# First norm taken by tokens beside the first projection tile, last norm split into a weight per tile and a factor per token

## The reference, cut to what matters

```python
def first_block(...):
    h = concatenate([meta_tokens, x], axis=1)        # 16 + 512 rows of 1024
    for i in range(2):
        hn = _rmsnorm(h, norm_attn[i])               # i == 0: the first norm
        h = h + mixer(hn, ...)                       # i == 0: starts with hn @ w_in_even
        h = h + _sq_relu_mlp(_rmsnorm(h, norm_mlp[i]), ...)
    return _rmsnorm(h, norm_final)[:, 16:]

def second_block(...):
    h = hybrid_layer(x, ...)     # ends: h = h + sigmoid(h @ w_ple_gate) * (p @ w_ple_proj)
    return rmsnorm(h, g_final)                       # the last norm

def rmsnorm(x, g):
    return x * rsqrt(mean(x * x, axis=-1) + EPS) * g
```

## Time and profile before

| | us |
|---|---|
| median of 3 runs | 2258.49 (2254.37 to 2258.91) |
| the profiled execution, its own time | 2258.82 |
| its span, first to last instruction | 2257.0 |
| PE busy | 2178.8 (97%) |
| POOL / DVE / ACT busy | 896.0 / 1167.3 / 788.6 |
| mean granted TensorE clock | 0.989 |

### The profile page before, as it was taken

How to read it: one execution, slowest core, us unless ns; L and a number is a source line. 1 busy time by engine, 2 the same in 40 slices (tenths; PEclk the granted TensorE clock), 3 DMA queues, 4 the chain that set the end, 5 groups by cost and what they waited for, 6 DMA issues and landing times.

```text
span 2257.0 us, 33166 instructions
## 1 busy us (share of the span) xinstructions
PE 2178.8 (97%) x13070; PEld 1837.5 (81%) x13070; DVE 1167.3 (52%) x1764; ACT 788.6 (35%) x1329; POOL 896.0 (40%) x404
## 2 busy tenths in 40 slices
PE   7999899999999989999999989999999999999996
PEld 6987699999999756788887878788878788887874
DVE  5558757742752266651154358656564554442224
ACT  3338733212323275332233322234423332222223
POOL 2321734333444344444444433333334444444442
PEclk9999999999999999999999999999999999999998
DMA  5620045323342600333333273323323233332321
GB/s 138 173 64 1 2 115 154 94 79 122 94 131 84 194 11 20 94 93 93 94 95 95 81 175 109 109 76 86 85 80 95 79 114 95 96 95 84 96 87 51
DMA packets 374312, 210.58 MB, mean 93 GB/s; under 512 B 26239, under 2 KB 367328, under 8 KB 373296
## 3 DMA queue, kind: packets, MB, share of 16 engines
q1 hardware_dynamic: 363526, 190.95, 29.9%
q10 hardware_dynamic: 10666, 17.92, 2.9%
HBM read 196.82 MB, written 15.40 MB: 94 GB/s over the span
## 4 chain that ended last, share of the span: by engine, by line
issue 55%; POOL 26%; PE 14%; DVE 2%; ACT 1%; POOLq 1%; DMA 0%; SPq 0%; DVEq 0%; ACTq 0%
POOL w_lo L796 25%; PE acc L870 2%; PE acc L871 2%; PE acc L872 2%; PE acc L951 2%; PE ops L989 2%; PE tps L973 1%; DVE probs L2069 1%; POOL probs L825 1%; PE ops L987 1%; PE ops L971 1%; PE tps L929 0%; POOLq L795 0%; DMA meta_in<-in_meta_tokens 0%; POOLq L140 0%
## 5 line engine op out<-in xcount | busy, mean ns | idle before, releaser
L796 POOL TENSOR_TENSOR w_lo<-raw,w_hi 128x1024 fp32r<-128x1024 f32 x328 | 804.0, 2451 | 1193.2 <-ACT w_hi L1347 1169.0
L1347 ACT ACTIVATE w_hi<-raw 128x1024 fp32r<-128x1024 f32 x327 | 346.6, 1060 | 1075.8 <-PE acc L872 1049.0
L870 PE MATMUL acc<-hr_hi,w_hi 128*128 128x512 f32 x1120 | 448.5, 400 | 6.1 <-DVE u_t L2605 4.9
L871 PE MATMUL acc<-hr_lo,w_hi 128*128 128x512 f32 x1120 | 444.0, 396 | 0.0
L872 PE MATMUL acc<-hr_hi,w_lo 128*128 128x512 f32 x1120 | 443.9, 396 | 0.0
L870 PE MATMUL acc<-hn_hi,w_hi 128*128 128x264 f32 (+1 forms) x896 | 265.1, 296 | 5.3 <-POOL w_lo L796 4.6
L871 PE MATMUL acc<-hn_lo,w_hi 128*128 128x264 f32 (+1 forms) x896 | 261.9, 292 | 0.0
L872 PE MATMUL acc<-hn_hi,w_lo 128*128 128x264 f32 (+1 forms) x896 | 261.6, 292 | 0.0
L870 PEld LDWEIGHTS acc<-hr_hi,w_hi 128*128 128x128 f32 x1120 | 211.2, 189 | 59.5 <-DVE u_t L2605 5.3
L872 PEld LDWEIGHTS acc<-hr_hi,w_lo 128*128 128x128 f32 x1120 | 211.2, 189 | 51.1
L871 PEld LDWEIGHTS acc<-hr_lo,w_hi 128*128 128x128 f32 x1120 | 211.3, 189 | 50.1 <-issue 0.7
(11 more groups left out here) (391 smaller groups left out, 3690.1 us busy)
## 6 DMA issues: line engine op xcount, KB each, us to landing
raw<-in_w_up SPq DMA_DIRECT2D x64, 512.0 KB, 4.0
raw<-in_w_down SPq DMA_DIRECT2D x64, 512.0 KB, 4.1
raw<-in_w_in SPq DMA_DIRECT2D x56, 512.0 KB, 3.9
raw<-in_w_ffn_gate SPq DMA_DIRECT2D x22, 512.0 KB, 3.8
raw<-in_w_ffn_up SPq DMA_DIRECT2D x22, 512.0 KB, 3.8
raw<-in_w_in_even SPq DMA_DIRECT2D x18, 512.0 KB, 8.0
raw<-in_w_ffn_down SPq DMA_DIRECT2D x16, 512.0 KB, 4.0
raw<-in_w_in_odd SPq DMA_DIRECT2D x10, 512.0 KB, 5.5
```

What stands on the lines that cost most here:

```text
L796: nc.gpsimd.tensor_tensor(w_lo[:, part], raw[:, slot], w_hi[:, part].bitcast(F32), ALU.subtract).then_inc(sems["lo"], T.up("lo"))
L870: mm(out, w_hi[:, part, w0 + k, :], xh, start=s0, stop=False)
L871: mm(out, w_hi[:, part, w0 + k, :], xl, start=False, stop=False)
L1347: fn(w_hi[:, n % 2], raw[:, n % 4], ACT.Copy).then_inc(sems["hi"], T.up("hi"))
```

## The change

At the start, the squares are taken on the token rows, where a sum over features is a sum along a partition: ACT squares each of the four row tiles and the meta rows with an accumulated sum (`sq_tok`). DVE puts the sums on the diagonal of 128x128 tiles, and PE multiplies them by `ones` to get them along the columns and on all partitions. `add_squares` is gone. The remaining transposes `turn_x(2)` to `turn_x(7)` are issued from inside unit 0, one ahead of each block. ACT splits unit 0's weights early and unit 1's between the seventh and eighth `hn_hi`. SP waits for x before it issues the load of unit 1.

At the end, ACT puts the weights on each tile of `h` right after its squares (`out_t`), PE transposes two such tiles in the next step of `ple`, behind the second gate tile, and DVE copies them to `out_sb`. After the last step, PE takes the sum as four products with one column, which leaves one number for each token on its partition. Sqrt and reciprocal are then of 128x4, and ACT and DVE each multiply two of the four row tiles of `out_sb`; ACT issues two of the transfers, SP the other two.

```diff
@@ SP
-            units(even_in, {3: setup_loads, 11: swap_heads, 12: bias_a_load})
+            units(even_in, {0: lambda: sp.wait_ge(sems["x_in"], T.at("x_in")), 3: setup_loads, 11: swap_heads, 12: bias_a_load})
...
+            for q in (1, 3):
+                T.saw("out_dve")
+                sp.wait_ge(sems["out_dve"], T.at("out_dve"))
+                load(out[q * P:(q + 1) * P, :], out_sb[:, q, :], "done")
@@ PE, unit()
+                    if ahead:
+                        ahead(0)
                     pe.wait_ge(sems["lo"], T.at("lo"))
                     T.unit += 1
                 for k in range(kt):
+                    if ahead and k:
+                        ahead(k)
@@ PE, start
-            def add_squares(k):
...
+            def turn_next(k):
+
+                if k + 2 < DT:
+                    turn_x(k + 2)
+
+            def token_stats():
+
+                T.saw("diag", 5)
+                pe.wait_ge(sems["diag"], T.at("diag"))
+                b = open_("o_")
+                for t in range(4):
+                    ins = mm(ops_[b][:, t * P:(t + 1) * P], ones[:], diag[:, t, :], start=True, stop=True)
+                close(ins, b, "o_")
+                b = open_("o_")
+                close(mm(ops_[b][:, 0:N_META], ones[0:N_META, :], diag_m[:], start=True, stop=True), b, "o_")
...
-            project(even_in, None, H_LO, None, after={
+            project(even_in, None, H_LO, token_stats, ahead=turn_next, after={
@@ PE, end
-            project(ple, None, H_LO)
-            stats(True)
-            T.saw("result", DT)
+            def ple_tile(t):
+
+                if t == 1:
+                    if steps:
+                        turn_result(2 * len(steps) - 2)
+                        turn_result(2 * len(steps) - 1)
+                    steps.append(t)
+
+            project(ple, None, H_LO, after_tile=ple_tile)
+            turn_result(DT - 2)
+            turn_result(DT - 1)
+            T.saw("sumsq", DT + 1)
+            pe.wait_ge(sems["sumsq"], T.at("sumsq"))
+            b = open_("o_")
             for q in range(4):
...
+                ins = mm(ops_[b][:, q:q + 1], sumsq[:, q * P:(q + 1) * P], ones[:, 0:1], start=True, stop=True)
+            close(ins, b, "o_")
@@ ACT, start
+            fn(small[:, 6:7], eps, ACT.Sqrt).then_inc(sems["metas"], T.up("metas"))
+            T.saw("x_in", 80)
+            act.wait_ge(sems["x_in"], T.at("x_in"))
+            square_tokens(0)
+            square_tokens(1)
+            T.saw("raw0", 16)
+            act.wait_ge(sems["raw0"], T.at("raw0"))
+            fn(w_hi[:, 0], raw[:, 0], ACT.Copy).then_inc(sems["hi"], T.up("hi"))
...
-                fn(sq[:, k % 2, :], h[:, k, :], ACT.Square).then_inc(sems["square"], T.up("square"))
...
+                if 1 <= k <= 3:
+                    square_tokens(k + 1)
+                if k == 6:
+                    next_hi(False)
+                    early.append(True)
@@ ACT, end
-                    squares(2 * m + t - 2, t, True)
+                    k = 2 * m + t - 2
+                    if k == DT - 2:
+                        fn(small[:, 6:7], eps, ACT.Sqrt).then_inc(sems["metas"], T.up("metas"))
+                    squares(k, t, True)
+                    fn(out_t[:, k, :], real(h[:, k, :]), ACT.Copy, scale=gains[:, 56 + k:57 + k]).then_inc(
+                        sems["result"], T.up("result"))
...
+            fn(rstd_tok, ops_[b][:, 0:4], ACT.Sqrt, bias=eps, scale=1.0 / D_MODEL).then_inc(
...
+            for q in (0, 2):
+                fn(out_sb[:, q, :], out_sb[:, q, :], ACT.Copy, scale=rstd_tok[:, q:q + 1]).then_inc(
+                    sems["out_act"], T.up("out_act"))
+                act.wait_ge(sems["out_act"], T.at("out_act"))
                 dma(out[q * P:(q + 1) * P, :], out_sb[:, q, :], "done")
@@ DVE, start
+            for t in range(4):
+                v.tensor_scalar(diag[:, t, :], ident[:], sq_tok[:, t:t + 1], None, ALU.mult).then_inc(
+                    sems["diag"], T.up("diag"))
@@ DVE, end
+            def keep_result(k):
+
+                b = result(T, "t_")
+                dve.wait_ge(sems[f"t_full{b}"], T.at(f"t_full{b}"))
+                v.tensor_copy(out_sb[:, :, k * P:(k + 1) * P], tps[b].rearrange("p (q c) -> p q c", q=4)).then_inc(
+                    sems[f"t_stored{b}"], T.up(f"t_stored{b}"))
+
             def embed(m, s, t, b):
+                if t == 2 and m:
+                    keep_result(2 * m - 2)
+                    keep_result(2 * m - 1)
...
-            stats(True)
-            for k in range(DT):
-                v.scalar_tensor_tensor(out_t[:, k, :], real(h[:, k, :]), gains[:, 56 + k:57 + k], real(rstd),
...
+            v.reciprocal(rstd_tok, rstd_tok).then_inc(sems["rstd_tok"], T.up("rstd_tok"))
...
+            for q in (1, 3):
+                v.tensor_scalar(out_sb[:, q, :], out_sb[:, q, :], rstd_tok[:, q:q + 1], None, ALU.mult).then_inc(
+                    sems["out_dve"], T.up("out_dve"))
```

More of the change, by code:

```diff
@@ L850, in close, with unit @@
                 T.saw(f"{kind}stored{b}")
-            def unit(b, kt, k0, src, first, last, ready=None, again=False):
+            def unit(b, kt, k0, src, first, last, ready=None, again=False, ahead=None):
                 x_hi, x_lo, width = src
@@ L873, in unit, with project @@
                 return ins
-            def project(pj, source=None, ready=None, after_first=None, after={}, after_tile=None):
+            def project(pj, source=None, ready=None, after_first=None, after={}, after_tile=None, ahead=None):
                 if ready:
                     T.saw(*ready)
-                at_first = [ready, after_first]
+                at_first = [ready, after_first, ahead]
                 def emit(m0, n):
@@ L892, in emit @@
                                 last = u == len(tl) - 1
-                                ins = unit(b, kt, k, source or SRC[src], u == 0, last, at_first[0])
+                                ins = unit(b, kt, k, source or SRC[src], u == 0, last, at_first[0], ahead=at_first[2])
                                 k += kt
@@ L1313, in _, with turn_result @@
                 pe.wait_ge(sems[kind], T.at(kind))
-            project(ple, None, H_LO)
-            stats(True)
-            T.saw("result", DT)
-            for q in range(4):
-                for f in range(2):
-                    if q == 0:
-                        pe.wait_ge(sems["result"], T.at("result", DT // 2 if f == 0 else 0))
-                    transposes("t_", [(lambda t, k=k: t[:, k * P:(k + 1) * P],
-                                       out_t[:, 4 * f + k, q * P:(q + 1) * P], 0) for k in range(4)])
+            steps = []
+            def turn_result(k):
+                T.saw("result")
+                pe.wait_ge(sems["result"], T.at("result"))
+                transposes("t_", [(lambda t, q=q: t[:, q * P:(q + 1) * P],
+                                   out_t[:, k, q * P:(q + 1) * P], 0) for q in range(4)])
+            def ple_tile(t):
[10 more added lines that the diff above has]
+            b = open_("o_")
+            for q in range(4):
+                ins = mm(ops_[b][:, q:q + 1], sumsq[:, q * P:(q + 1) * P], ones[:, 0:1], start=True, stop=True)
+            close(ins, b, "o_")
         @block.scalar
@@ L1334, in wait_last @@
                     act.wait_ge(sems[kind], T.at(kind))
+            early = []
             def next_hi(within):
+                if early:
+                    early.clear()
+                    return
                 n = T.unit + 1
@@ L1546, in _, with token_stats @@
                 fn(hn_hi[:, k, :], h[:, k, :], ACT.Copy, scale=gains[:, k:k + 1]).then_inc(sems["h_hi"], T.up("h_hi"))
-                if k > 1:
-                    T.saw("summed")
-                    act.wait_ge(sems["summed"], T.at("summed"))
-                fn(sq[:, k % 2, :], h[:, k, :], ACT.Square).then_inc(sems["square"], T.up("square"))
-                if k == 4:
-                    T.saw("raw0", 16)
-                    act.wait_ge(sems["raw0"], T.at("raw0"))
-                    fn(w_hi[:, 0], raw[:, 0], ACT.Copy).then_inc(sems["hi"], T.up("hi"))
+                if 1 <= k <= 3:
[3 more added lines that the diff above has]
+                    early.append(True)
+            def token_stats():
+                for out in (rstd[:, 0:SEQ], rstd[:, SEQ:LEN]):
+                    b = result(T, "o_")
+                    act.wait_ge(sems[f"o_full{b}"], T.at(f"o_full{b}"))
+                    fn(out, ops_[b][:, 0:out.shape[1]], ACT.Sqrt, bias=eps, scale=1.0 / D_MODEL).then_inc(
+                        sems[f"o_stored{b}"], T.up(f"o_stored{b}"))
+                T.saw("rstd")
             def even_duty(m, s, t, b):
```

65 lines of the change are left out of this document (35 added, 30 removed).

## The result

The changed kernel takes 2261.33 us (median of 22 runs, 2254.79 to 2263.33), the kernel before 2257.02 (22 runs beside them): a ratio of 1.0017, 95% interval 1.0009 to 1.0024. That is no change by the bound of 0.2% named in the prediction, on its slow side: 3.8 us more, between 2.0 and 5.4. The prediction was 2260, from a kernel before at 2258.5 (the median of 3 runs then known). The profiled execution has its own time of 2262.83, a span of 2261.1 and a mean granted clock of 0.987.

A forecast was written before the change was run, and what follows sets the result against it. TensorE, busy 97% of the span, was taken as the bound, with waits over several engines at both ends. 2257.0 + 11.5 (start) - 9.95 (tail) = 2258.6 as a span, 2260 as time; range 2252 to 2266.

The forecast's parts named there:

- signs named as wrong: Tiles every 3 us, unit 1 before 45 or after 50, longer last-projection steps, or output transfers not back to back.
- x and unit 0's start: Start: x there at 9.57 as before, first hn_lo slowed beside POOL, unit 0 starting at 16.2 instead of 30.36.
- The chain in unit 0: Unit 0: a chain without overlap, 4.2 us a tile at the low clock, last matmul 4.7 us later than before.
- Rival (a): Unit 0: the clock rises inside it, start +7.7, time about 2256.6, still no change; chance 0.18.
- Behind unit 0: From unit 0's last matmul to unit 1: sums, reciprocal and store no longer hidden, 7.45 us, 5.3 more than before.
- Rival (c): Faster: the reciprocal stays hidden behind unit 0 (start +4.7, time 2253.6) or the end gives its best; chance 0.14.
- Unit 1 at the low clock: Unit 1: starts at the low clock after PE's wait of about 4 us, rises after 3 us, 1.5 us lost.
- Rival (b): Slower: the clock stays low through unit 1, net +7.4, time 2266; chance 0.19.
- The start as a whole: Start through unit 1: predicted +11.5 us, with bounds +6.2 and +17.4.
- The steps of the last projection: Last projection: eight transposes cost 0.9 us, falling into a wait in the second and third step, paid in the last.
- The tail: From the last projection's end to the kernel's end: predicted -9.95 us, with bounds -11.3 and -8.4.
- The rule on transposes and the clock: Skill's rule that transposes do not count as clock activity; it would make unit 0's low clock certain, leaving the sum unchanged.

The follow-up runs named there:

- the sums inside: Changed kernel with the diagonals' five products and the two Sqrts moved into unit 0, so the reciprocal starts behind the last hn_lo: 2254.57 us, 0.9995.
- the bank first: Changed kernel with DVE emptying the bias banks ahead of the reciprocal of rstd and the first store: 2253.40 us, 0.9991.
- the version that keeps the clock: Changed kernel with seven extra, overwritten products on PE ahead of the third bias product, where it idles: 2254.76 us, 0.9997.
- The tail alone: Kernel before with only the change's last norm, the start left as before: 2247.48 us, 0.9960.

## Why the prediction was right, point by point

None of the signs named as wrong came: tiles took 4.00 us, unit 1 started at 47.71, the steps of the last projection kept their length, and the transfers ran back to back.

**x and unit 0's start.** 9.57 was taken for the first transpose; it was 10.12. It is not the change: with the unchanged start it was 9.81, 9.91 and 10.19. Relative to it, unit 0 came after 6.3 us (6.6 predicted), and the collision of `hn_lo` with POOL was there, 1.46 for 0.76.

**The chain in unit 0** was right in kind, 4.00 us for a tile instead of 4.2, since six matmuls at the low clock took 1.49 and not 1.65. The clock rose at 40.1, 3.7 us into the dense end. The last matmul came 30.2 us behind the first transpose; 31.3 was predicted. Rival (a), a rise inside unit 0, did not happen; it does when the chain is open (at 20.9 with `hn_lo` ahead of the copy) or when the sums fill one of its gaps (just before 35.09).

**Behind unit 0:** 7.42 from the last matmul to unit 1 (7.45 predicted), 3.88 of it PE's wait (4 predicted). Rival (c) assumed this away; the versions with the sums inside and the bank first show that it takes an edit.

**Unit 1 at the low clock** is the term that was mis-sized: 2.8 us instead of 1.5, by the version that keeps the clock. I let the clock rise after 3 us of dense work, as in the earlier trace rows; it took from 47.71 to 53.8. Rival (b) had this mechanism, but with a clock low through the whole of unit 1 and 7.4 net; it was a third of the way there. The start as a whole came to 11.5 by the first pair of traces, exactly the sum, since the tile (1.2 us less than predicted) and the clock (1.2 more) erred in opposite directions: that this sum is exact is luck.

**The steps of the last projection.** Eight transposes took 1.04, hidden in the second and third step (PE's first long matmuls of the steps lie 15.2 us apart, as before) and paid in the last: 0.9, as predicted. DVE's `h` met POOL for 1.10 us instead of 1.93, which the prediction did not have and which hid.

**The tail.** -9.95 was the sum. The first pair of traces has -11.2 and +0.9, or -10.3. The clock fell only at about 2252, behind the transposes; in the second trace of the same kernel it fell earlier: the last four and the short products took 1.12 and 1.71 instead of 0.66 and 1.24, and the tail was -9.5. Issue to end: 7.0 (6.75 predicted). (The 25.6 in the prediction counts from the end of PE's last long product, the table's 26.0 from its start.) The tail alone measured -9.0 (-12.2 to -6.1).

**The number.** 2260 against 2261.33 looks closer than it is. The forecast started from 2258.5, and the kernel before turned out at 2257.02; as a difference it was +1.5, and the runs say +3.8 (2.0 to 5.4). "No change" holds with 0.17% against a bound of 0.2%.

**What stays open.** +11.7 by the traces with either start (mean of 148.6, 147.9, 148.1 less that of 137.0, 137.1, 136.0, 136.1) and -9.9 for the tail make +1.8 or so; the runs say 3.8 (2.0 to 5.4). Whether the middle is 2 us longer with a late start could not be told: six traces with a start of 143 to 149 have 2135.3 to 2143.4 (mean 2140.0), four with the start of before 2136.1 to 2140.0 (mean 2137.9). The means differ by just the missing 2 us, but single traces scatter by more.

The rule on transposes and the clock that the prediction weighed meets a second row here. In the version with all transposes last, PE did nothing but transposes from 2231.99 to 2236.97, and the granted clock was 0.50 from 2232 to 2235, 0.96 in the next microsecond and 1.00 behind it:

```profile
2234.00:2235.00 1.00, 1.00 (x5) 0.86 (x6) 0.66 (x1) 0.00 (x0) 0.00 (x0) 0.50 0.07 16
2235.00:2236.00 1.00, 0.64 (x6) 0.43 (x5) 0.93 (x2) 0.00 (x0) 0.00 (x0) 0.96 0.00 0
```

So this case's traces do not agree with the Trainium skill (TensorE: Matmul & The Clock Gate, Part 4: PE-mode transpose), by which transposes don't count as PE being busy in the same way.

## What to carry to other kernels

Interleaving two loops brings work forward only if no engine's list puts the next tile's step ahead of this tile's: here one exchange on DVE was worth 11 to 13 us, more than the whole tail. When an early start moves a statistic behind the unit that used to hide it, look for what really stands in the waiter's way (a bank, not the reciprocal) and move that. Split a change with two ends and time the halves: "no change" was 14.0 us lost and 9.0 gained, by versions with one half each.

## What the hardware showed that I had not expected

- The granted clock can fall after the wait is over: 2.43 us idle, then 1.3 us of dense matmuls at 0.12 us each, then 3.4 us at 0.22.
- With PE busy 2.5 of every 4.0 us it stayed at 1.2 GHz for 24 us (16.4 to 40.1). How long dense work ran until the rise differed: 3.7 us until 40.1, 6.1 until 53.8, and 4.7 until 20.9 in the version with `hn_lo` first.
- At the start the PEclk column says 1.00 whatever the clock; only durations tell.
- `hn_lo` takes 0.76 us alone, 1.46 to 1.60 as the first one beside POOL's subtraction, 2.43 later in unit 0 with `hn_lo` first and 2.65 in the earlier trace rows; the subtraction itself takes 2.35 to 2.45; `band_row`, with two inputs from SBUF as well, 1.67 instead of 0.68. The reciprocal of one input beside the same subtraction took 3.45, as alone. The Trainium skill (GPSIMD Engine Reference, 1. Specifications) names the same pair, GpSimd and VectorE instructions with two SBUF inputs; the traces agree.
- x landed between 9.57 and 10.61 us over fourteen traces, and the middle of the kernel varied by 8.8 us, so one pair of traces can't settle a difference of 2 us.
